# Two transformer-like blocks on one core: the norms at the ends of block and layer, reordered

## The reference, cut to what matters

```python
# first block, end of its mixing part: residual, LayerNorm, then the router of 32 experts
x = _layer_norm(DN_ALPHA * x + merged @ w_out[l], ln_g[l, 0], ln_b[l, 0])
lg = (xs @ wr_g) + br_g             # 4 group logits
le = (xs @ wr_e) + br_e             # 32 expert logits; experts follow

def _layer_norm(x, g, b):
    mu = mean(x); var = mean(square(x - mu))
    return (x - mu) * rsqrt(var + LN_EPS) * g + b

# second block, each of two layers
h = rmsnorm(x, norm_pre[l])         # opens a layer; for layer 1 it is computed at the end of layer 0
...
x = x + rmsnorm(merged @ w_out[l], norm_post[l])

def rmsnorm(x, g):
    return x * rsqrt(mean(x * x) + EPS) * g
```

## Time and profile before

| | |
|---|---|
| median of the runs shown | 2440.09 us |
| the profiled execution | 2443.96 us, of it 2442.1 us span |
| PE busy | 2202.9 us (90%) |
| DVE busy | 1360.9 us (56%) |
| ACT busy | 906.1 us (37%) |
| block end | about 706 to 771 us of the span |
| end of layer 0 | about 1742 to 1810 us |
| end of layer 1 | about 2406 to 2442 us |

### The profile page before, as it was taken

The page is one execution under the profiler, slowest core; times in us unless marked ns, Lnnn a source line. Parts: engine busy times, 40 slices in busy tenths (PEclk is TensorE's granted clock), DMA queues, the critical chain, the costliest instruction groups (busy, mean ns, idle before and its releaser), DMA issues. The chain is left out here.

```text
span 2442.1 us, 30103 instructions
## 1 busy us (share of the span) xinstructions
PE 2202.9 (90%) x11232; PEld 1664.2 (68%) x11232; DVE 1360.9 (56%) x2391; ACT 906.1 (37%) x1538; POOL 122.2 (5%) x153
## 2 busy tenths in 40 slices
PE   6798998899996999991899989999979998899997
PEld 4587765556776666650777768888757766788886
DVE  2652446856445655544345585964444456778544
ACT  3521233123232666654333433332333334233323
POOL 0000002200000232320000000000000000000000
PEclk8885999999997999995999989999989999999999
DMA  5220431231423899975332113322423222141313
GB/s 162 88 74 1 125 93 54 62 100 44 124 91 143 317 366 358 369 269 184 99 100 66 65 61 104 99 87 87 143 78 103 79 62 65 57 143 64 108 48 112
DMA packets 218989, 296.45 MB, mean 121 GB/s; under 512 B 48861, under 2 KB 183085, under 8 KB 210617
## 3 DMA queue, kind: packets, MB, share of 16 engines
q1 hardware_dynamic: 213722, 286.09, 35.0%
q0 software_dynamic: 5120, 8.40, 1.1%
HBM read 283.12 MB, written 22.07 MB: 125 GB/s over the span
## 5 line engine op out<-in xcount | busy, mean ns | idle before, releaser
L1556 PE MATMUL acc<-x_hi,w_hi 128*128 128x512 f32 x1432 | 579.3, 405 | 19.5 <-DVE w_lo L1507 16.2
L1557 PE MATMUL acc<-x_lo,w_hi 128*128 128x512 f32 x1432 | 566.0, 395 | 0.0
L1558 PE MATMUL acc<-x_hi,w_lo 128*128 128x512 f32 x1432 | 565.2, 395 | 0.0
L1477 ACT CAST w_hi<-raw 128x1024 fp32r<-128x1024 f32 x179 | 186.9, 1045 | 621.5 <-PE acc L1558 587.0
L1507 DVE TENSOR_TENSOR w_lo<-raw,w_hi 128x1024 fp32r<-128x1024 f32 x174 | 212.7, 1224 | 292.6 <-ACT w_hi L1477 289.3
L1556 PEld LDWEIGHTS acc<-x_hi,w_hi 128*128 128x128 f32 x1432 | 273.8, 191 | 84.2 <-DVE w_lo L1507 17.2
L1558 PEld LDWEIGHTS acc<-x_hi,w_lo 128*128 128x128 f32 x1432 | 273.2, 191 | 60.3
L1557 PEld LDWEIGHTS acc<-x_lo,w_hi 128*128 128x128 f32 x1432 | 274.0, 191 | 57.9 <-issue 2.0
L1176 DVE TENSOR_TENSOR w_lo<-wgu,w_hi 128x1024 fp32r<-128x1024 f32 x128 | 151.0, 1220 | 61.3 <-ACT w_hi L1135 60.7
L1135 ACT CAST w_hi<-wgu 128x1024 fp32r<-128x1024 f32 x128 | 127.9, 1047 | 38.6 <-DMA wgu<-in_moe_w_up 33.2
L1108 PE MATMUL ps<-wd,y 128*64 128x512 f32 x256 | 116.7, 598 | 0.7 <-DVE y L1192 0.7
(11 more groups left out here) (554 smaller groups left out, 3357.7 us busy)
## 6 DMA issues: line engine op xcount, KB each, us to landing
raw<-in_w_in SPq DMA_DIRECT2D x60, 1024.0 KB, 5.5
raw<-in_w_gate SPq DMA_DIRECT2D x40, 1024.0 KB, 5.5
wgu<-in_moe_w_gate SPq DMA_DIRECT2D x32, 1024.0 KB
wgu<-in_moe_w_up SPq DMA_DIRECT2D x32, 1024.0 KB
wd<-in_moe_w_down SPq DMA_DIRECT2D x32, 1024.0 KB, 5.3
raw_b<-in_w_branch SPq DMA_DIRECT2D x56, 256.0 KB, 2.8
room<-in_w_out SPq DMA_DIRECT2D x3, 2048.0 KB, 8.4
y_t<-in_w_out SPq DMA_DIRECT2D x3, 2048.0 KB, 10.8
```

The costliest lines, as they stand in the source:

```text
L1477: self.nc.scalar.copy(self.w_hi[n % 2], self.weights(n)).then_inc(self.rounded, 1)
L1556: pe.matmul(acc, hi, tile.hi[:, k, :], start=(k == 0), stop=False)
L1557: pe.matmul(acc, hi, tile.lo[:, k, :], start=False, stop=False)
L1558: mm = pe.matmul(acc, lo, tile.hi[:, k, :], start=False, stop=(k == KT - 1))
```

## The change

At both layer ends the squares of all four first halves move ahead of the loop; DVE adds 1e-6 to each of these four sums early (L3176 after the change). The root of a tile then takes the sum of the second half as input and that early sum as its bias, and the root of `pre` takes a constant tile `eps` as bias: no DVE instruction stands between a square and its root any more. In the loop, ACT and DVE take the steps of `pre` first and the rounding of a turned tile last. At the block end the DVE instruction that adds product and rows also puts out the row's sum, a small DVE instruction (L3303) makes the mean of the two, and ACT's Copy pass goes. ACT's `channels(0)` and `channels(1)` stand ahead of the square of tile 3, and PE does `route(1)` ahead of `turn(2)`, `turn(3)` ahead of `route(2)`.

```diff
@@ layer_end, ACT
+                act.wait_ge(eps_ready, 1)
+                for i in range(NT):
+                    nc.scalar.activation(sq[:, 0:512], o.ps[:, i, :], ACT.Square, scale=D ** -0.5, accum_out=st[:, i, 0:1]
+                                         ).then_inc(squared, 1)
+                    act.wait_ge(squared, i + 1)
                 for s in range(steps):
                     if pre is not None and 0 <= s - 1 < NT:
                         act.wait_ge(rowed, s)
-                        run(nc.scalar.activation(sq[:], room[:, s - 1, :], ACT.Square, scale=D ** -0.5,
-                                                 accum_out=st[:, s - 1, 4:5]))
-                        act.sem_inc(pre_squared, 1)
+                        run(nc.scalar.activation(sq[:], room[:, s - 1, :], ACT.Square, accum_out=st[:, s - 1, 4:5]))
+                        nc.scalar.activation(st[:, s - 1, 6:7], st[:, s - 1, 4:5], ACT.Sqrt, bias=eps[:], scale=1.0 / D
+                                             ).then_inc(pre_rooted, 1)
+                    if s < NT:
+                        act.wait_ge(o.acc, s + 1)
+                        run(nc.scalar.activation(sq[:, 512:1024], o.ps[:, s + 4, :], ACT.Square, scale=D ** -0.5,
+                                                 accum_out=st[:, s, 1:2]))
+                        act.wait_ge(biased, s + 1)
+                        nc.scalar.activation(st[:, s, 3:4], st[:, s, 1:2], ACT.Sqrt, bias=st[:, s, 2:3]).then_inc(rooted, 1)
                     if pre is not None and 0 <= s - 2 < NT:
                         act.wait_ge(turned, s - 1)
                         ...
-                    if s < NT:
-                        for half in range(2):
-                            ...
-                        act.sem_inc(squared, 1)
-                        act.wait_ge(var, s + 1)
-                        nc.scalar.activation(st[:, s, 3:4], st[:, s, 2:3], ACT.Sqrt).then_inc(rooted, 1)
-                    if pre is not None and 0 <= s - 1 < NT:
-                        act.wait_ge(pre_var, s)
-                        nc.scalar.activation(st[:, s - 1, 6:7], st[:, s - 1, 5:6], ACT.Sqrt).then_inc(pre_rooted, 1)
@@ layer_end, DVE
+                for i in range(NT):
+                    dve.wait_ge(squared, i + 1)
+                    nc.vector.tensor_scalar(st[:, i, 2:3], st[:, i, 0:1], 1e-6, None, ALU.add).then_inc(biased, 1)
                 for s in range(steps):
-                    if pre is not None and 0 <= s - 1 < NT:
-                        dve.wait_ge(pre_squared, s)
-                        nc.vector.tensor_scalar(st[:, s - 1, 5:6], st[:, s - 1, 4:5], 1e-6, None, ALU.add).then_inc(pre_var, 1)
...
@@ block_end, PE
                 route(0)
+                route(1)
                 turn(2)
-                route(1)
                 turn(3)
@@ block_end, ACT
                 for i in range(NT):
-                    act.wait_ge(summed, i + 1)
-                    run(nc.scalar.activation(sq[:], room[:, i, :], ACT.Copy, scale=-1.0 / D, accum_out=st[:, i, 0:1]))
-                    act.sem_inc(mean, 1)
+                    if i == NT - 1:
+                        channels(0)
+                        channels(1)
+                    act.wait_ge(mean, i + 1)
                     run(nc.scalar.activation(sq[:], room[:, i, :], ACT.Square, bias=st[:, i, 0:1], accum_out=st[:, i, 1:2]))
...
@@ block_end, DVE
                         run(nc.vector.scalar_tensor_tensor(room[:, i, cols], room[:, i, cols], ALPHA, o.ps[:, i + 4 * half, :],
-                                                           ALU.mult, ALU.add))
-                    dve.sem_inc(summed, 1)
+                                                           ALU.mult, ALU.add, accum_out=st[:, i, 4 + half:5 + half]))
+                    nc.vector.tensor_scalar(st[:, i, 0:1], st[:, i, 4:5], st[:, i, 5:6], -1.0 / D, ALU.add, ALU.mult).then_inc(mean, 1)
```

More of the change, by code:

```diff
@@ L3088, in layer_end @@
         gb, sq, st = c.sb(ctx, "gains", [P, 2, D]), c.sb(ctx, "sq", [P, D]), c.sb(ctx, "stat", [P, NT, 8])
+        eps = c.sb(ctx, "eps", [P, 1])
         space = merged.rearrange("p k s -> p (k s)").rearrange("p (i d) -> p i d", i=NT)
@@ L3092, in layer_end @@
         rows_in = [c.sem("rows_in") for _ in range(NT)]
-        (squared, var, rooted, rowed, pre_squared, pre_var, pre_rooted, h_ready, turned, x_rounded, x_split, chain, act_chain) = (
-            c.sem(x) for x in ("squared", "var", "rooted", "rowed", "pre_squared", "pre_var", "pre_rooted", "h", "turned",
-                               "x_rounded", "x_split", "dve", "act"))
+        (eps_ready, squared, biased, rooted, rowed, pre_rooted, h_ready, turned, x_rounded, x_split, chain, act_chain) = (
+            c.sem(x) for x in ("eps", "squared", "biased", "rooted", "rowed", "pre_rooted", "h", "turned", "x_rounded",
+                               "x_split", "dve", "act"))
         gains = [post] if pre is None else [post, pre]
@@ L3168, in _ @@
                 run = Chain(dve, chain)
+                nc.vector.memset(eps[:], 1e-6).then_inc(eps_ready, 1)
                 o.dve(dve)
@@ L3196, in _ @@
                         dve.wait_ge(rooted, s + 1)
-                        run(nc.vector.reciprocal(st[:, s, 3:4], st[:, s, 3:4]))
+                        run(nc.vector.reciprocal(st[:, s, 5:6], st[:, s, 3:4]))
                         for half in range(2):
                             cols = slice(half * 512, half * 512 + 512)
-                            run(nc.vector.scalar_tensor_tensor(scaled[:, s % 2, cols], o.ps[:, s + 4 * half, :], st[:, s, 3:4],
+                            run(nc.vector.scalar_tensor_tensor(scaled[:, s % 2, cols], o.ps[:, s + 4 * half, :], st[:, s, 5:6],
                                                                gb[:, 0, cols], ALU.mult, ALU.mult))
@@ L3203, in _ @@
                         nc.vector.tensor_tensor(room[:, s, :], room[:, s, :], scaled[:, s % 2, :], ALU.add).then_inc(rowed, 1)
+                    if pre is not None and 0 <= s - 2 < NT:
+                        for half in range(2):
+                            k = slice(4 * half, 4 * half + 4)
+                            dve.wait_ge(x_rounded, 2 * (s - 2) + half + 1)
+                            nc.vector.tensor_tensor(x_lo[:, k, (s - 2) * P:(s - 1) * P], turned_rows(s - 2, half),
+                                                    x_hi[:, k, (s - 2) * P:(s - 1) * P].bitcast(F32), ALU.subtract
+                                                    ).then_inc(x_split, 1)
 def block_end(c, stream, merged, x_hi, x_lo, w_out, raw, room, x_from, x_t, x_dram, gain, bias, wr, wr_bias, lg):
@@ L3215, in block_end @@
         rows_in = [c.sem("rows_in") for _ in range(NT)]
-        eps_ready, summed, mean, rooted, ready, turned, in_channels, logits, chain, act_chain = (
-            c.sem(x) for x in ("eps", "summed", "mean", "rooted", "ready", "turned", "in_channels", "logits", "dve", "act"))
+        eps_ready, mean, rooted, ready, turned, in_channels, logits, chain, act_chain = (
+            c.sem(x) for x in ("eps", "mean", "rooted", "ready", "turned", "in_channels", "logits", "dve", "act"))
         c.to_fetch += [(gb[:, j, :], one.partition_broadcast(P), gains_in) for j, one in enumerate((gain, bias))]
@@ L3275, in _ @@
                 for i in range(NT):
-                    act.wait_ge(summed, i + 1)
-                    run(nc.scalar.activation(sq[:], room[:, i, :], ACT.Copy, scale=-1.0 / D, accum_out=st[:, i, 0:1]))
-                    act.sem_inc(mean, 1)
+                    if i == NT - 1:
+                        channels(0)
+                        channels(1)
+                    act.wait_ge(mean, i + 1)
                     run(nc.scalar.activation(sq[:], room[:, i, :], ACT.Square, bias=st[:, i, 0:1], accum_out=st[:, i, 1:2]))
                     nc.scalar.activation(st[:, i, 2:3], st[:, i, 1:2], ACT.Sqrt, bias=eps[:], scale=1.0 / D).then_inc(rooted, 1)
-                    if i >= 2:
-                        channels(i - 2)
                 channels(2)
```

## The result

The changed kernel took 2426.39 us, the median of four runs (2424.75 to 2434.96), beside 2442.28 us of four runs of the kernel before: a ratio of 0.9936, with a 95% interval of 0.992 to 0.9953. Two later comparisons gave 0.9925 (0.9904 to 0.9946) and 0.9946 (0.9928 to 0.9963). By these ratios the change makes the kernel 13 to 18 us faster (by the medians 13.4 to 17.0). The profiled execution, the longest of the four, took 2434.96 us, of it 2433.2 span; that is 9.0 us less than the profiled execution of before.

A forecast was written before the change was run, and what follows sets the result against it. Bounds taken: the ACT-DVE round at layer 0's end, PE's order and speed at the block end, the last tile's chain after PE at layer 1's end. 9.0 + 1.2 + 0.2 = 10.4 us off 2440.09 gives 2429.7; range 2424.5 to 2434.7.

The forecast's parts named there:

- the clock rival: Block end: PE's clock stays up through last turn and routes; gain there 5.3 us, total 14.5, 2425.6 us; chance 0.13.
- the three ends: Gains at the block end 1.2 us, end of layer 0 9.0 us, end of layer 1 0.2 us.
- The round: End of layer 0: loop between ACT and DVE shrinks from 8.73 to 5.93 us per round; gain 9.0 us.
- All three conditions: End of layer 0: `x_lo` fits DVE's wait, the product's root comes in time, PE's 5.6 us product stays below 5.93.
- the rival of rounds that shrink less: End of layer 0: `x_lo` does not fit or roots come late; half the saving, total 5.6 us, 2434.5 us; chance 0.13.
- The block end: Block end: `turn(3)` starts at 761.2 instead of 762.36, clock low as before; gain 1.2 us, ends 0.5 and 1.4.
- the cost of the sum on DVE and the mean: Block end, DVE's path to tile 3: together 0.4 us added, with ends of 0.2 and 1.1.
- The end of layer 1: From ACT's read to the reciprocal 0.35 us instead of 0.56; gain 0.2 us.
- The opening of layer 1: Stage after layer 0 opens about 6 us at low clock; 2 to 3 us longer or shorter, worth up to 1.5 us.

The follow-up runs named there:

- a4_order_only: Changed kernel, but at the layer ends both additions of 1e-6 stand again on DVE between a square and its root; 2428.75 us, ratio 0.993 to before.
- b1_fill_layer: Changed kernel plus 33 matmuls whose result nobody reads, in PE's pauses at the end of layer 0; 2427.66 us, ratio 0.9938 to before.
- a1_again: The changed kernel once more, in five rounds against the kernel before, with a second profile; 2427.34 us, ratio 0.9925.

## Why the prediction was right

The time, 2426.4 us, lies in the range, and the direction was right. But the difference is larger than the sum, 13 to 18 us instead of 10.4, and two of its three intervals (11.5 to 19.5, 13.2 to 23.5, 9.0 to 17.6) leave 10.4 out. That the time is only 3.3 us from the forecast is in part luck: the base of the forecast, 2440.09, was a low draw of three. By the time alone the clock rival, at 2425.6, would have been the better forecast. What bears the prediction out are the rows of the three ends.

**The round** was forecast as 5.93 us and is 5.94; the gain of 9.0 is 8.95 in the profile. All three conditions for it held, and the rival of rounds that shrink less is refuted: `x_lo` fits. `a4_order_only` shows the parts: the order gives 6.9 of the 8.95 us, the biases 2.0. The price of that rival, 4.2 us, was half of three equal savings; half of the 8.95 found would be 4.5.

**The block end** was mis-sized in one term, the cost of the sum on DVE and the mean. I took 0.4 us; the half's start to that of the next large instruction is 0.87 us (755.51 to 756.38) and was 0.84: 0.03. The read of the accumulator is there, as the Trainium skill has it ("VectorE: DVE Perf Modes", "Two Vector instructions with no wait between them"), and takes 0.08 us; it and the mean fit into the wait of the instruction for its predecessor. A further 0.1 us was a small wait that the prediction did not see: before, DVE's work on tile 3 began 1.29 us behind the instruction ahead of it, on the end of the root (757.91), and now it begins 1.21 us behind. So the gain is 1.6, not 1.2. That the root of tile 3 is not the bound holds after the change (it ends at 758.85, DVE gets to it at 759.09).

**The end of layer 1**: 0.2 forecast, 0.20 found.

**The clock rival** had 0.13, as one case for every execution. That was the wrong form. I read from the trace of before that turns and routes never bring the clock back, from one stretch of 12 us. `a4_order_only` and `b1_fill_layer` show it coming back in just such work, and their block end is 4.7 us shorter than before, near the 5.3 of the rival. It differs from one execution to the next: two of seven profiles with this order. Weighed so, it adds 0.9 us to the 1.6, but seven profiles are few, and three of them (the first of the changed kernel, `a1_again` and `a4_order_only`) are of the longest execution of their version. I also argued about PE's pause, for and against this rival, and the pause does not place the fall: behind the last product the clock fell after 4.8 us with a pause of 1.24 us on the way (before), and after 4.7 to 4.9 us with none (the five long ones). What went ahead of the fall in all of them is the change from the product to turns and routes.

**The opening of layer 1** at the low clock lasted 4.9 us (to 1808.0) instead of 6.1, worth some 0.5 us, inside the 1.5 that I allowed.

**What stays open.** 10.8 us by the rows of the three ends, 0.9 for the clock and 0.5 for the opening make 12.2. Over the three comparisons the 16 executions of the changed kernel have a median of 2429.2 us, the 34 of before one of 2444.5: 15.3. The 12.2 lie within two of the three intervals and below the third. No profile shows where the 3 us between are, and the profiles are not placed to show it: the three of the changed kernel are of executions of 2433.48 to 2436.25 us, all among its six longest. Over all 16 the mean granted clock goes with the time: 0.931 to 0.933 in the six longest, 0.933 to 0.937 in the ten others. So the rest may well be clock too; a profile of one of the shorter executions would tell. Executions of one kernel differ by up to 14.5 us (before: 2436.70 to 2451.18), and the stretch ahead of the first of the three ends, the same code in all, ended between 753.8 and 757.0 us in the profiles.

## What to carry to other kernels

Where ACT and DVE pass one small number to and fro for each tile, write down the round instruction by instruction. Moving everything out from between a square and its root that the root does not need gave over three times what cutting two tiny instructions gave. A pass that is taken off one engine and a reordering of another may each be worth nothing until both are done: look which wait ends last after each. And when PE has only thin work at the end of a stage, its clock is part of the cost, of this stage and of the next one's opening; compare such stages by several profiles, not by one.

## What the runs showed of the hardware

- Behind the last product, under turns and routes, the granted clock fell from 1.00 to 0.50 after 4.5 to 4.9 us in all eleven profiles without extra matmuls there, with a pause of PE on the way or with none. Such work ran 12 us at 0.50 in the kernel before, and yet in two profiles of the new order the clock, fallen in 759 to 760, was back at 1.00 in 763 to 764 and in 762 to 763, and fell again in 766 to 767, before the last route was over. Twelve matmuls of 512 columns among it held 1.00 to the last route in both profiles that have them.
- A DVE instruction that also sums its row takes 0.69 us for 128x512, as without the sum, and its read 0.08; ACT's read takes 0.18 to 0.21.
- A root with its bias from a tile takes 0.29 us instead of 0.20, and saves the 0.3 us of a handover to DVE and back.
